# Expert products in native float32 on four column tiles of TensorE, with eight neighbouring weight rows on each partition

## The chip, the cores and the metric

One core of a Trainium2 chip runs the whole layer in one launch. The metric is the device time of one execution in microseconds (us). A core has a matrix engine (TensorE, PE in the rows; its weight loads are PEld), a vector engine (VectorE, DVE), a scalar engine (ScalarE, ACT), a general engine (GpSimd, POOL), and SyncE (SP), which here only issues DMAs. The engines meet at semaphores: an instruction adds to one when it is done, another waits until it has a value.

## The reference, cut to what matters

The layer normalises its input, runs attention and a state-space mixer side by side, projects, normalises, and then sends the tokens through an expert-choice mixture of experts. There are two sequences (256 and 512 tokens), width 1024, 16 experts of inner width 1024. Each expert picks 2 x 256/16 = 32 tokens of the first sequence and 64 of the second, 96 in all.

```python
def _expert_choice(h, w_router, w_gate, w_up, w_down):
    n_tok, d = h.shape
    cap = CAPACITY_FACTOR * n_tok // N_EXPERTS
    aff = jax.nn.softmax((h @ w_router).astype(jnp.float32), axis=-1)
    gate, idx = lax.top_k(aff.T, cap)
    xe = h[idx]
    hid = jax.nn.silu(jnp.einsum("ecd,edf->ecf", xe, w_gate)) * jnp.einsum("ecd,edf->ecf", xe, w_up)
    ye = jnp.einsum("ecf,efd->ecd", hid, w_down) * gate[..., None].astype(h.dtype)
    return jnp.zeros_like(h).at[idx.reshape(-1)].add(ye.reshape(-1, d))
```

All is float32. The weights of the experts are 16 x 3 x 4 MB = 201 MB, nearly all that the kernel reads. After the experts a per-layer embedding term and a last layer norm follow.

## The kernel before

Each engine has its own program. Up to some 620 us the layer runs up to the router, the choice of tokens and the per-layer embedding units (`ple_unit`, 12 of them, L1777); then comes the expert stage, and from 1190 us the last norm.

In the expert stage the 96 chosen rows of an expert are gathered from DRAM by GpSimd (`gather`, L635) to `xe`, turned by eight transposes on TensorE (`rows_turn`, L1865), and copied out as the stationary operand `xeT`. The weights stream past it: for each of 8 row blocks of 128 and each half of 512 columns a product of 128 x 96 by 128 x 512 is added into PSUM (`chunk`, L1873).

The products run on operands in parts. A weight piece lands in `raw` (1 MB: two row blocks, 128 x 2048); ScalarE copies it to `high` in the shorter format float32r (`split`, called through `copy`, L698), and VectorE subtracts to get `low` (`split`, L1327). The same is done to `xeT` and `hidT`. A product is then high x high, high x low and low x high: three float32r matmuls (L1880 to L1882) instead of one float32 matmul. An expert's weights are 12 pieces (4 of gate, 4 of up, 4 of down), and `raw`, `high` and `low` are rings of 6. SP loads the next piece when the split of the piece six before is done (`s_low`, L519); ScalarE splits when TensorE has used the ring's slot (`s_used`).

The order on TensorE for expert e: `gate(e)`, `hid_turn(e-1)` (eight transposes of the hidden rows), `up(e)`, `rows_turn(e+1)`, `down(e-1)`. ScalarE applies silu, VectorE multiplies gate and up (`hidden`, L1358) and scales the output by the gate value (`ye_out`, L1364, operation on L1368). GpSimd adds the 96 rows of 4 KB to DRAM (`scatter`, L656), and after the last one SP reads all back for the norm (L525 to L527).

Row `k*128 + p` of a weight matrix goes to partition p (`"e (k p) f -> e p k f"`, L496), so that a piece takes two single rows of 4 KB for each partition, 512 KB apart in DRAM.

Other products are native float32 matmuls: the per-layer units (L1792), the output projection (L1760), and the router (L1832: eight row blocks into 16 output columns, 512 and 256 moving columns).

Of the kernel before, what the change touches and what calls it, by code (L numbers as in the profile page):

```python
# [20 lines left out]
ALU = mybir.AluOpType  # L21
# [7 lines left out]
P = 128  # L29
# [17 lines left out]
NB = 6  # L47
# [18 lines left out]
def hymba_layer(nc, A, consts, out_prompt, out_sample):  # L66
# [7 lines left out]
    CAP = CAPP + CAPS  # L74
    PADW = TP * P + TS * P + 6
# [6 lines left out]
    with ctx:  # L82
# [43 lines left out]
        gateT = sb("gateT", [CAP, NE])  # L126
        idxT = sb("idxT", [CAP, NE], I32)
        idx_now = sb("idx_now", [CAP, 2], I32)
# [55 lines left out]
        xaf = xa[:, :, :].rearrange("p t c -> p (t c)")  # L184
# [16 lines left out]
        xeT = [over(f"xeT{i}", "xa", i * KD * CAP, [P, KD, CAP]) for i in range(2)]  # L201
        hidT = [over(f"hidT{i}", "xa", (2 + i) * KD * CAP, [P, KD, CAP]) for i in range(2)]
        hid = xaf[0:CAP, 4 * KD * CAP:4 * KD * CAP + D]
        ye = xaf[0:CAP, 4 * KD * CAP + D:4 * KD * CAP + 2 * D]

        CH = 2 * D
        raw = [late[:, j * CH:(j + 1) * CH] for j in range(NB)]
        where = [("ring", 4), ("ring", 8), ("xT", 0), ("xT", 4), ("ring", 0), ("mix", 0)]
        high = [over(f"high{j}", b, o * D, [P, CH]) for j, (b, o) in enumerate(where)]
        where[3] = ("gb_in", -2)  # L210
        low = [over(f"low{j}", b, (o + 2) * D, [P, CH]) for j, (b, o) in enumerate(where)]
# [97 lines left out]
        s_raw = [sem(f"s_raw{j}") for j in range(NB)]  # L309
        s_high = sem("s_high")  # L310
        s_low = sem("s_low")
        s_used = sem("s_used")
        s_xeT_h = sem("s_xeT_h")
# [3 lines left out]
        s_hT_h = sem("s_hT_h")  # L317
# [55 lines left out]
        QC = D // (2 * P)  # L373
        FIRST, PER = 2 * QC, 3 * QC

        def buf(i):
            return i % NB

        def buf0(n):
            return (n + NB - FIRST % NB) % NB  # L380

        def seq(e, i):
            return PER * e + (FIRST - PER + i)

        def landed(e, i):
            before = [buf0(n) for n in range(FIRST)].count(buf(i))
            return 16 * (PER // NB) * (e - 1) + 16 * (before + 1 + i // NB)

# [34 lines left out]
        def _(sp):  # L423
# [72 lines left out]
            wg = A["w_e_gate"][0].rearrange("e (k p) f -> e p k f", p=P)  # L496
# [3 lines left out]
            def load(j, w, e, q):  # L500
                sp.dma_start(raw[j].rearrange("p (k c) -> p k c", k=2),
                             w[e, :, 2 * q:2 * q + 2, :]).then_inc(s_raw[j], 16)
# [1463 lines left out]
```

## Time and profile before

| | |
|---|---|
| median of 3 runs | 1227.28 us (1225.72 to 1228.53) |
| span of the profiled execution | 1227.0 us |
| TensorE busy in it | 1125.2 us, 92% |
| VectorE, ScalarE, GpSimd busy | 850.3, 602.9, 364.2 us |
| moved by DMA | 253.86 MB, 207 GB/s over the span |
| mean granted clock of TensorE | 0.965 of full |

The profile follows one execution. The span goes from the first to the last instruction of it. Busy shares are means over stages that differ much, so the expert stage is read by itself below. In a timeline row the first number is the start, the second the time from the start of the group's first instruction to the end of its last, and `x8` the number of instructions in it. The end of a matmul is modelled, so its pace is read from starts.

### The profile page before, as it was taken

The numbers are of one execution on the slowest core, as the hardware profiler recorded it, in microseconds if no ns is written. First come the engines' busy times: TensorE is split into PE (matmuls) and PEld (weight loads), VectorE is DVE, ScalarE is ACT, GpSimd is POOL, SyncE is SP. The second block draws the span as 40 slices with busy tenths as digits, with TensorE's granted clock in tenths as the row PEclk, the third lists the DMA queues.
The fourth block names the chain that finished last, engine by engine and source line by source line (L and its number), as shares of the span: only waits on it lengthen the run. The fifth ranks groups of instructions, "written<-read, shape, count | busy, mean of one in ns | idle before, by whom it ended". The sixth has DMA issues, their size and how long they took to land.

```text
span 1227.0 us, 13573 instructions
## 1 busy us (share of the span) xinstructions
PE 1125.2 (92%) x4706; PEld 736.3 (60%) x4706; DVE 850.3 (69%) x1026; ACT 602.9 (49%) x741; POOL 364.2 (30%) x275
## 2 busy tenths in 40 slices
PE   5999869789998999999999999999999999999950
PEld 3568758565665454344466777777777777777630
DVE  5436783557778154273358888988888889988738
ACT  1143244456575110110256676687666776787522
POOL 0007992244544000000100333322333333322313
PEclk9999889979999999999999999999999999999985
DMA  9010100300000930200559999999999999999815
GB/s 331 6 69 4 66 1 1 103 1 1 1 1 2 317 136 35 94 26 26 175 214 332 384 382 389 390 379 390 384 395 381 385 389 395 382 386 380 311 29 202
DMA packets 74886, 253.86 MB, mean 207 GB/s; under 512 B 7384, under 2 KB 9304, under 8 KB 74848
## 3 DMA queue, kind: packets, MB, share of 16 engines
q1 hardware_dynamic: 69440, 234.49, 50.1%
q0 software_dynamic: 5408, 18.88, 5.7%
q8 instruction: 22, 0.36, 0.1%
q14 instruction: 16, 0.13, 0.0%
HBM read 237.62 MB, written 15.73 MB: 206 GB/s over the span
## 4 chain that ended last, share of the span: by engine, by line
PE 80%; DVE 9%; POOL 5%; issue 2%; ACT 2%; DMA 1%; SPq 0%; ACTq 0%; DVEq 0%; POOLq 0%
PE ps L1880 15%; PE ps L1882 14%; PE ps L1881 14%; PE ps L1792 7%; PE ps L1760 7%; PE ps L1558 4%; PE ps L1664 2%; PE ps L1679 2%; PE ps L1552 2%; PE ps L1861 2%; PE ps L1797 2%; DVE xT L1451 1%; DVE ring L1206 1%; PE ps L1790 1%; PE ps L1655 1%
## 5 line engine op out<-in xcount | busy, mean ns | idle before, releaser
L1327 DVE TENSOR_TENSOR low<-late,high 128x2048 fp32r<-128x2048 f32 x192 | 427.1, 2283 | 31.5 <-ACT high L698 31.5
L698 ACT ACTIVATE high<-late 128x2048 fp32r<-128x2048 f32 x192 | 354.9, 1914 | 24.0 <-DMA late<-in_w_e_up 23.7
L661 POOL COPY idx_now<-idxT 96x1 int32 (+1 forms) x30 | 132.7, 4423 | 375.3 <-DVE xa L1368 203.2
L1880 PE MATMUL ps<-high,xeT 128*96 128x512 f32 x528 | 210.8, 399 | 6.8 <-issue 4.8
L1882 PE MATMUL ps<-high,xeT 128*96 128x512 f32 x528 | 208.9, 396 | 0.0
L1881 PE MATMUL ps<-low,xeT 128*96 128x512 f32 x528 | 208.4, 395 | 0.0
L1880 PEld LDWEIGHTS ps<-high,xeT 128*96 128x96 f32 x528 | 86.0, 163 | 43.3 <-issue 6.1
L1882 PEld LDWEIGHTS ps<-high,xeT 128*96 128x96 f32 x528 | 85.9, 163 | 37.7 <-issue 0.5
L1881 PEld LDWEIGHTS ps<-low,xeT 128*96 128x96 f32 x528 | 86.0, 163 | 36.3 <-issue 0.3
L1880 PE MATMUL ps<-high,hidT 128*96 128x512 f32 x240 | 95.5, 398 | 2.3 <-DVE low L1327 2.3
L1882 PE MATMUL ps<-high,hidT 128*96 128x512 f32 x240 | 94.2, 393 | 0.0
L1881 PE MATMUL ps<-low,hidT 128*96 128x512 f32 x240 | 94.0, 392 | 0.0
L1792 PE MATMUL ps<-ring,xT 128*128 128x512 f32 x192 | 85.6, 599 | 0.0
L1792 PEld LDWEIGHTS ps<-ring,xT 128*128 128x128 f32 x192 | 35.5, 190 | 49.3 <-issue 49.3
L698 ACT ACTIVATE xT<-ps 128x512 f32<-128x512 f32 (+1 forms) x48 | 22.3, 512 | 70.2 <-PE ps L1773 43.2
L1285 DVE TENSOR_TENSOR mix<-mix,ps 128x512 f32<-128x512 f32 x12 | 8.2, 687 | 67.7 <-ACT mix L892 67.6
L698 ACT ACTIVATE hidT<-ps 128x384 fp32r<-128x384 f32 x30 | 13.1, 489 | 84.1 <-PE ps L1861 84.1
L822 ACT ACTIVATE ring<-ps,att 128x512 f32<-128x512 f32 (+1 forms) x48 | 29.4, 612 | 48.9 <-DVE att L1175 48.8
L892 ACT ACTIVATE mix<-ps 128x512 f32<-128x512 f32 x12 | 7.2, 597 | 93.2 <-PE ps L1797 93.2
L1880 PEld LDWEIGHTS ps<-high,hidT 128*96 128x96 f32 x240 | 38.7, 161 | 18.2 <-DVE low L1327 2.8
L1882 PEld LDWEIGHTS ps<-high,hidT 128*96 128x96 f32 x240 | 38.7, 161 | 16.9
L1881 PEld LDWEIGHTS ps<-low,hidT 128*96 128x96 f32 x240 | 38.8, 162 | 15.5
(255 smaller groups left out, 1858.1 us busy)
## 6 DMA issues: line engine op xcount, KB each, us to landing
late<-in_w_e_gate SPq DMA_DIRECT2D x64, 1024.0 KB, 6.9
late<-in_w_e_up SPq DMA_DIRECT2D x64, 1024.0 KB, 8.0
late<-in_w_e_down SPq DMA_DIRECT2D x64, 1024.0 KB, 8.1
ring<-in_w_in SPq DMA_DIRECT2D x3, 2048.0 KB, 9.1
ring<-in_w_ple_gate SPq DMA_DIRECT2D x2, 2048.0 KB, 11.5
ring<-in_w_in SPq DMA_DIRECT2D x3, 1024.0 KB, 13.0
x_rows<-xa POOLq DMA_DIRECT2D x6, 512.0 KB, 2.9
acc_rows<-mix POOLq DMA_DIRECT2D x12, 256.0 KB, 2.3
```

Of the source, the lines that this page charges most:

```text
L661: return nc.gpsimd.tensor_copy(idx_now[:, col:col + 1], idxT[:, bass.ds(e, 1)])
L698: return nc.scalar.activation(o, i, ACT.Copy)
L822: nc.scalar.activation(prob[:, u % 4, 0:L], ps[:, u % 3, 0:L], ACT.Exp, bias=att[:, 0, u:u + 1], scale=HD ** -0.5, accum_out=att[:, 1, u:u ...
L1327: nc.vector.tensor_tensor(low[j], raw[j], high[j], ALU.subtract).then_inc(s_low, 1)
L1552: last = nc.tensor.matmul(bank[:, 0:272], lhs[k], wkv[:, k, :], start=(k == 0), stop=(k == KD - 1))
L1558: last = nc.tensor.matmul(bank, lhs[k], slotk[0][:, k, :], start=(k == 0), stop=(k == KD - 1))
L1664: last = nc.tensor.matmul(ps[:, 4, :], kvd[:, a + b, P:2 * P], probT[G % 2][:, b, :], start=(b == 0), stop=(b == n - 1))
L1760: last = nc.tensor.matmul(ps[:, 4 + 2 * (t % 2) + h, :], lhs, w[:, k, :], start=(k == 0), stop=(k == KD - 1))
L1792: nc.tensor.matmul(ps[:, b, :], xT[:, k, t * P:(t + 1) * P], w[:, k, :], start=False, stop=(k == KD - 1))
L1880: nc.tensor.matmul(o, lhs[0][:, k, :], high[j][:, c], start=(k == 0), stop=False)
L1881: nc.tensor.matmul(o, lhs[0][:, k, :], low[j][:, c], start=False, stop=False)
L1882: last = nc.tensor.matmul(o, lhs[1][:, k, :], high[j][:, c], start=False, stop=(k == KD - 1))
```

## The change

The three parts, both splits and the rings go. Gate, up and down are native float32 products. The 96 tokens are three groups of 32. A product takes 32 tokens as the stationary operand and writes 32 PSUM partitions, `32*j` to `32*j+31`; j = 0..3 stands for the quarter of the inner width (or of the output width) that it computes, so that four products of a group write four column tiles of the array. Gate and up of a quarter are one product of 2 x 256 = 512 moving columns; down has 256.

The hidden rows so lie as 128 partitions (quarter, token) x 3 groups x 256, and six full transposes turn them. The output lies the same way, hence 3 scatters of 128 rows of 1 KB for each expert (`acc_quarters`), with indices `4*token + quarter` made for it (`idx4`, `jcol`) by 24 small products with the identity, beside the one transpose for the gather's indices.

Gate and up weights go to the partitions by eight neighbouring rows (row `8*p + k`), and `rows_turn` takes every eighth column of the gathered rows to match. Weights land in six slots of 2 MB: four hold a quarter of the row blocks of gate and up, two hold a half of down. SP loads into a slot when the products that used it are done (`s_ug`, `s_ud`).

Before the stage, the last per-layer unit writes its second product to bank 1 and waits for one more sum. ScalarE and VectorE keep silu, the copies out of PSUM, the product and the scaling.

```diff
-        CH = 2 * D
-        raw = [late[:, j * CH:(j + 1) * CH] for j in range(NB)]
-        high = [over(f"high{j}", b, o * D, [P, CH]) for j, (b, o) in enumerate(where)]
-        low = [over(f"low{j}", b, (o + 2) * D, [P, CH]) for j, (b, o) in enumerate(where)]
+        acc_quarters = acc_rows.rearrange("t (j c) -> (t j) c", j=CT)
+        gu_w = [slot[j].rearrange("p (w k c) -> p w k c", w=2, k=2) for j in (3, 4, 5, 0)]
+        dn_w = [slot[j].rearrange("p (k c) -> p k c", k=4) for j in (1, 2)]
...
-            wg = A["w_e_gate"][0].rearrange("e (k p) f -> e p k f", p=P)
-            wu = A["w_e_up"][0].rearrange("e (k p) f -> e p k f", p=P)
+            wg = A["w_e_gate"][0].rearrange("e (p k) f -> e p k f", p=P)
+            wu = A["w_e_up"][0].rearrange("e (p k) f -> e p k f", p=P)
             wd = A["w_e_down"][0].rearrange("e (k p) f -> e p k f", p=P)
+            def load_gu(e, q):
+                for i, w in enumerate((wg, wu)):
+                    sp.dma_start(gu_w[q][:, i], w[e, :, 2 * q:2 * q + 2, :]).then_inc(s_guw[q], 16)
+            def load_dn(e, d):
+                sp.dma_start(dn_w[d], wd[e, :, 4 * d:4 * d + 4, :]).then_inc(s_dnw[d], 16)
             sp.wait_ge(s_gs, NG)
-            for n in range(NB):
-                load(buf0(n), (wg, wu)[n // QC], 0, n % QC)
+            for q in range(3):
+                load_gu(0, q)
             sp.wait_ge(s_o, NT)
             sp.dma_start(slotk[2], wpg[:, :, 512:D]).then_inc(s_slot[2], 16)
+            load_gu(0, 3)
+            sp.wait_ge(s_pg, NT)
+            load_dn(0, 0)
...
+            sp.wait_ge(s_pg, 2 * NT)
+            load_dn(0, 1)
             for q in range(QC):
-                sp.wait_ge(s_low, seq(NE, q) - NB + 1)
-                load(buf(q), wd, NE - 1, q)
+                sp.wait_ge(s_ug, q + 1)
+                load_gu(1, q)
+            with sp.Fori(2, NE) as e:
+                for q in range(QC):
+                    sp.wait_ge(s_ug, 4 * (e - 1) + q + 1)
+                    load_gu(e, q)
+                for d in range(2):
+                    sp.wait_ge(s_ud, 2 * (e - 2) + d + 1)
+                    load_dn(e - 1, d)
...
             def scatter():
-                pool.indirect_dma_start(acc_rows, bass.IndirectOffsetOnAxis(ap=idx_now[:, 1:2], axis=0),
-                                        ye, None, compute_op=ALU.add).then_inc(s_scat, 16)
+                for i in range(NG3):
+                    pool.indirect_dma_start(acc_quarters,
+                                            bass.IndirectOffsetOnAxis(ap=idx_now[:, 1 + i:2 + i], axis=0),
+                                            ye[:, i, :], None, compute_op=ALU.add).then_inc(s_scat, 16)
...
             def ye_out(e, at_e, first=False):
+                dve.wait_ge(s_ud, 2 * (e + 1))
                 if not first:
-                    dve.wait_ge(s_scat, 16 * e)
+                    dve.wait_ge(s_scat, 16 * NG3 * e)
+                for i in range(NG3):
+                    last = nc.vector.tensor_scalar(ye[:, i, :], ps[:, DN + i, 0:256], gate4[:, i, at_e], None,
+                                                   ALU.mult)
...
+                if u == 2 * NT - 1:
+                    pe.wait_ge(s_base, u)
...
+            for v, src in enumerate((topf, topv)):
+                for i in range(NG3):
+                    c = (1 + v * NG3 + i) * NE
+                    for j in range(CT):
+                        last = nc.tensor.matmul(ps[32 * j:32 * (j + 1), 5, c:c + NE], src[:, i * 32:(i + 1) * 32],
+                                                ident[0:NE, 0:NE], start=True, stop=True)
...
-                        nc.tensor.matmul(o, lhs[0][:, k, :], high[j][:, c], start=(k == 0), stop=False)
-                        nc.tensor.matmul(o, lhs[0][:, k, :], low[j][:, c], start=False, stop=False)
-                        last = nc.tensor.matmul(o, lhs[1][:, k, :], high[j][:, c], start=False,
-                                                stop=(k == KD - 1))
+            def gate_up(e):
+                pe.wait_ge(s_xeT, e + 1)
+                if not isinstance(e, int) or e:
+                    pe.wait_ge(s_hid, e)
                 for q in range(QC):
+                    pe.wait_ge(s_guw[q], 32 * (e + 1))
+                    for i in range(2):
+                        k = 2 * q + i
+                        for g in range(NG3):
+                            for j in range(CT):
+                                last = nc.tensor.matmul(
+                                    ps[32 * j:32 * (j + 1), GU + g, :].rearrange("p (w c) -> p w c", w=2),
+                                    xeT[:, k, 32 * g:32 * (g + 1)],
+                                    gu_w[q][:, :, i, 256 * j:256 * (j + 1)], start=(k == 0), stop=(k == KD - 1))
+                    last.then_inc(s_ug, 1)
+
+            def down_half(e, d, src):
+                pe.wait_ge(s_dnw[d], 16 * (e + 1))
+                for i in range(4):
+                    k = 4 * d + i
+                    for g in range(NG3):
+                        for j in range(CT):
+                            last = nc.tensor.matmul(ps[32 * j:32 * (j + 1), DN + g, 0:256],
+                                                    src[:, k, 32 * g:32 * (g + 1)],
+                                                    dn_w[d][:, i, 256 * j:256 * (j + 1)],
+                                                    start=(k == 0), stop=(k == KD - 1))
+                last.then_inc(s_ud, 1)
...
             with pe.Fori(2, NE - 1) as e:
-                gate(e)
+                pe.wait_ge(s_xeT, e + 1)
                 hid_turn(e - 1)
-                up(e)
+                gate_up(e)
                 pe.wait_ge(s_hT, e)
                 rows_turn(e + 1)
-                down(e - 1)
+                down(e - 1, hidT)
```

The order for expert e is now `hid_turn(e-1)`, `gate_up(e)`, `rows_turn(e+1)`, `down(e-1)`.

## Rows read from the trace of the kernel before

**Rows 1.** The page: the chain that ended last, by engine and by line.
```profile
PE 80%; DVE 9%; POOL 5%; issue 2%; ACT 2%; DMA 1%; SPq 0%; ACTq 0%; DVEq 0%; POOLq 0%
PE ps L1880 15%; PE ps L1882 14%; PE ps L1881 14%; PE ps L1792 7%; PE ps L1760 7%; PE ps L1558 4%; PE ps L1664 2%; PE ps L1679 2%; PE ps L1552 2%; PE ps L1861 2%; PE ps L1797 2%; DVE xT L1451 1%; DVE ring L1206 1%; PE ps L1790 1%; PE ps L1655 1%
```
**Rows 2.** Window: length; busy PE, PEld, DVE, ACT, POOL; clock, DMA, GB/s.
```profile
760.00:770.00 10.00, 10.00 (x50) 7.19 (x49) 6.45 (x6) 6.42 (x6) 4.12 (x2) 1.00 1.03 384
```
**Rows 3.** The page's groups: the two splits of the weights.
```profile
L1327 DVE TENSOR_TENSOR low<-late,high 128x2048 fp32r<-128x2048 f32 x192 | 427.1, 2283 | 31.5 <-ACT high L698 31.5
L698 ACT ACTIVATE high<-late 128x2048 fp32r<-128x2048 f32 x192 | 354.9, 1914 | 24.0 <-DMA late<-in_w_e_up 23.7
```
**Rows 4.** Timeline of TensorE, steady part: products, then eight transposes.
```profile
1142.57 0.39 PE L1881 MATMUL ps<-low,xeT 128*96 128x512 f32 x1
1142.80 0.39 PE L1882 MATMUL ps<-high,xeT 128*96 128x512 f32 x1
1143.03 0.82 PE L1861 MATMUL ps<-cst,xa 96*128 96x96 f32 x8
1143.63 0.46 PE L1880 MATMUL ps<-high,xeT 128*96 128x512 f32 x1
```
**Rows 5.** Timeline of SP: the gate loads of two experts, one after the other.
```profile
762.79 11.63 SPq L501 DMA_DIRECT2D late<-in_w_e_gate  x4
...
797.36 11.63 SPq L501 DMA_DIRECT2D late<-in_w_e_gate  x4
```
**Rows 6.** The router's float32 products: their piece of the chain, then weight loads (timeline).
```profile
501.07 10.42 PE ps L1832 x32
...
501.44 0.10 PEld L1832 LDWEIGHTS ps<-xT,wr 128*16 128x16 f32 x1 [0.33 <-issue]
501.87 0.10 PEld L1832 LDWEIGHTS ps<-xT,wr 128*16 128x16 f32 x1 [0.33 <-issue]
```
**Rows 7.** Timeline of weight loads: eight of 6-column transposes, and the next.
```profile
86.52 0.57 PEld L1500 LDWEIGHTS ps<-cst,late 6*128 6x128 f32 x8 [0.36 <-issue]
87.10 0.19 PEld L1531 LDWEIGHTS ps<-xh_a,wh 128*128 128x128 f32 x1
```
**Rows 8.** Waits of the SP queue: line, who, us in total, times, longest.
```profile
SPq L501 <- DVE low L1327: 549.2, 186, 95.5
```
**Rows 9.** Windows, columns as above: 2 KB rows, 4 KB rows, scatter, gather.
```profile
412.00:414.00 2.00, 2.00 (x6) 0.91 (x5) 0.00 (x0) 0.00 (x0) 0.00 (x0) 1.00 1.08 373
...
930.00:932.00 2.00, 2.00 (x10) 1.39 (x9) 2.00 (x2) 0.62 (x1) 2.00 (x1) 1.00 1.03 412
...
942.00:944.00 2.00, 2.00 (x10) 1.42 (x9) 2.00 (x2) 2.00 (x2) 0.00 (x0) 1.00 1.04 281
...
956.00:958.00 2.00, 2.00 (x11) 1.37 (x10) 2.00 (x2) 2.00 (x2) 0.00 (x0) 1.00 1.03 315
```
**Rows 10.** Timeline of GpSimd: issue of a scatter.
```profile
936.33 1.46 POOL L657 DMA_INDIRECT acc_rows<-xa,idx_now  x1 [0.80 <-POOL idx_now L661]
```
**Rows 11.** The stage's start in the timeline; then the chain's last scaling.
```profile
612.33 0.69 DVE L1286 SCALAR_TENSOR_TENSOR mix<-xa,mix 128x512 f32<-128x512 f32 x1
...
619.55 1.88 PE L1797 MATMUL ps<-gb_in,kvd 128*128 128x512 f32 x4
...
620.87 0.80 PE L1880 MATMUL ps<-high,xeT 128*96 128x512 f32 x1
...
1187.75 1.29 DVE xa L1368
```
**Rows 12.** Timeline of TensorE after a wait, and the window around it.
```profile
646.28 0.55 PE L1880 MATMUL ps<-high,xeT 128*96 128x512 f32 x1 [2.02 <-DVE xeT L1347]
646.62 0.63 PE L1881 MATMUL ps<-low,xeT 128*96 128x512 f32 x1
647.05 0.63 PE L1882 MATMUL ps<-high,xeT 128*96 128x512 f32 x1
...
645.00:650.00 5.00, 3.72 (x10) 2.47 (x10) 4.80 (x5) 5.00 (x4) 0.97 (x1) 0.66 0.97 350
```

More of the change, by code:

```diff
@@ L308, in hymba_layer @@
         s_xeT = sem("s_xeT")
[L309 to L313, printed above, removed]
+        s_guw = [sem(f"s_guw{q}") for q in range(4)]
+        s_dnw = [sem(f"s_dnw{d}") for d in range(2)]
+        s_ug = sem("s_ug")
+        s_ud = sem("s_ud")
         s_hs = sem("s_hs")
@@ L368, in hymba_layer, with gate_bank, p_bank @@
             n0 += n - 1
[L373 to L387, printed above, removed]
+        def gate_bank(u):
+            return 2 * (u % 2)
+        def p_bank(u):
+            return 1 if u == 2 * NT - 1 else 2 * (u % 2) + 1
+        GU, DN, TURN = 3, 0, 6
         DT, ANEG, ACUM, EA, WDEC, CD, W1, W2 = range(8)
@@ L939, in silu, with rows_out @@
-            def silu(e, first=False):
-                act.wait_ge(s_used, (QC if first else seq(e, QC)))
-                nc.scalar.activation(hid, ps[0:CAP, 0:2, :].rearrange("p b c -> p (b c)"),
-                                     ACT.Silu).then_inc(s_hs, 1)
+            def rows_out(e):
+                act.wait_ge(s_xeT_p, e + 1)
+                for half in range(2):
+                    last = copy(xeT[:, 4 * half:4 * half + 4, :],
+                                ps[:, TURN + half, 0:4 * CAP].rearrange("p (k c) -> p k c", k=4))
+                last.then_inc(s_xeT, 1)
@@ L956, in _ @@
[L956 to L970 removed]
+            rows_out(0)
+            sigmoid(2 * NT - 1)
@@ L971, in _ @@
+            silu(0)
+            rows_out(1)
             with act.Fori(1, NE - 1) as e:
[L972 to L974 removed]
                 silu(e)
[L976 to L983 removed]
@@ L1425, in stats_half @@
+            ye_out(0, slice(0, 1), first=True)
+            with dve.Fori(2, NE) as e:
+                hid_out(e - 1, hidT)
+                hidden(e)
+                ye_out(e - 1, bass.ds(e - 1, 1))
+            hid_out(NE - 1, xeT)
+            ye_out(NE - 1, slice(NE - 1, NE))
             def stats_half(t, half):
@@ L1886, in gate @@
-            def gate(e):
+                for i in range(NG3):
+                    for b in range(2):
+                        last = nc.tensor.transpose(ps[:, TURN + b, i * P:(i + 1) * P],
+                                                   hid[:, i, b * P:(b + 1) * P], ident)
+                last.then_inc(s_hT_p, 1)
+            def gate_up(e):
                 pe.wait_ge(s_xeT, e + 1)
-                pe.wait_ge(s_hs, e)
+                if not isinstance(e, int) or e:
+                    pe.wait_ge(s_hid, e)
@@ L1898, in down @@
+            def down(e, src, mid=None):
                 pe.wait_ge(s_hT, e + 1)
-                if not first:
+                if not isinstance(e, int) or e:
                     pe.wait_ge(s_ye, e)
-                for q in range(QC):
-                    if q == QC // 2 and mid:
-                        mid()
-                    chunk(hidT, 4, q, buf(2 * QC + q), seq(e + 1, 2 * QC + q))
-            pe.wait_ge(s_idx, 2)
+                down_half(e, 0, src)
+                if mid:
+                    mid()
+                down_half(e, 1, src)
```

287 lines of the change are left out of this document (71 added, 216 removed).

## The prediction

> **What bounds the kernel now.** The chain of waits on the page comes first: 80% of it is TensorE, and the three product lines of the experts (L1880 to L1882) hold 43% of the span, some 528 us [rows 1]. Read next what the expert stage looks like in ten-microsecond stretches: TensorE is busy for all 10 us at full clock, and the DMA engines are at a share of 1.03 as well [rows 2]. So two resources are full at once, and whichever stays full after the change decides. VectorE and ScalarE are busy, but not full, and the page's groups say with what: 192 splits of 2.28 us and 192 copies of 1.91 us [rows 3]. They end no wait of TensorE in the steady part. The timeline of TensorE gives the price of a product: 0.23 us from one to the next, and eight transposes in 0.60 us [rows 4]. The loads of one expert follow those of the expert before by 34.57 us [rows 5]. An expert has 8 row blocks x 2 halves x 3 weights x 3 parts = 144 products: 144 x 0.2295 = 33.05 us, two sets of transposes 1.20, together 34.25; 0.32 us is left over. TensorE's own work sets the period, with the DMA queue close behind.
>
> **Products of the change.** For gate and up an expert gets 8 x 3 x 4 = 96 products of 512 columns, for down 96 of 256. They are native float32. What such a product costs is seen at the router: its 16 products are 32 records in 10.42 us; the loads of the 512-column ones stand 0.43 us apart [rows 6]. So one product is two records, one after the other: 2 x 0.43 = 0.86 us at 512 columns, and (10.42 - 16 x 0.43)/16 = 0.22 us a record, 0.43 us a product, at 256. Served one at a time, an expert would be 96 x 0.86 + 96 x 0.43 = 123.8 us. No row shows products of different column tiles next to each other: the router's 16 output columns all lie in one tile, and its records don't overlap. So the cost is bounded by 123.8 us (nothing overlaps) and 123.8/4 = 31.0 us (four tiles always run together). I take 31.0: the four products of a group write four different quarters of the output and share no weights in the array, and adjacent records on this engine already run back to back without a gap [rows 4, 6]. This is the choice on which all else hangs; the rivals hold the other ends.
>
> A second floor is the spacing of small pairs of load and product: eight transposes of 6 columns take 0.58 us until the next load, 0.072 us a pair [rows 7], with 128-column loads where the change loads 32. Four tiles together ask for a pair each 0.43/4 = 0.107 us (gate and up) and 0.054 us (down). By that floor the 192 down pairs cost up to 13.8 instead of 10.3 us, so 0 to 3.5 us per expert; I take 0.5, since the load of 16 columns is 0.10 us against 0.19 of 128 [rows 6, 7].
>
> Transposes: eight stay (0.60), the other eight become six (0.45). Kept change-overs 0.32. Period of TensorE: 31.0 + 0.5 + 1.05 + 0.32 = 32.9 us against 34.57.
>
> **What leaves the other engines.** The 384 splits and copies go, with all the ring's waits on L1327. They are worth nothing by themselves, as TensorE did not wait for them in steady state. The wait of SP moves from the split to the consuming products (s_ug, s_ud): now 549 us of SP's waiting ends with a split [rows 8]. The new buffers hold six pieces of 2 MB, a whole expert, instead of six of 1 MB, so a load is issued as much as one expert ahead. Queued behind each of SP's new waits are the later loads only; the order of loads is that of use.
>
> **DMA.** An undisturbed stretch moves 412 GB/s in rows of 4 KB; 2 KB rows moved 373; the stretches with the scatter and the gather fall to 281 and 315 [rows 9]. With 16 engines a 4 KB row costs 159 ns and a 2 KB row 88, so 71 ns per 2 KB and 17 ns fixed; by the same line an 8 KB row would cost 302 ns, 434 GB/s (an estimate; no row is that long). Gate and up are 8.39 MB an expert: 20.4 us now, 19.3 by that line, so 0 to 1.1 us saved; I take 0.5. If the 8 KB are still moved as two rows, nothing is saved. The scatter goes from 96 rows of 4 KB to 384 of 1 KB: 288 more pieces on 16 engines at 17 ns are 0.3 us; if its slow stretch of some 3 us goes by pieces, it is 4 x 3 = 12 us, 9 more. I take 0.3, the price of short rows seen elsewhere. The DMA need is at most 34.57 us now (share near 1), 34.4 after. TensorE at 32.9 would outrun it, but starts with expert 0 and half of its down weights already in place: from 621 us on 190.8 MB remain, 15.2 experts' worth, 15.2 x 34.4 = 523 us, to about 1149 with 5 us of gaps at the start. POOL issues three scatters of 1.46 us [rows 10] instead of one, 2.9 us more in a period where it idles.
>
> [...]
>
> **The sum**, against the profiled execution's span, 1227.0 us (the median of the runs is 1227.28, so no correction). The products of the experts start at 620.8 us [rows 11]. 24 small products for the indices and gates by quarter, two records each: 48 x 0.072 = 3.5 us, to 624.3. The last per-layer unit now waits for one more sum of VectorE before its second product; that sum ends at 613.0 and the product starts at 619.55 [rows 11], so 6 us cover it. 16 x 32.9 = 526.4, to 1150.7. Gaps: after expert 0 TensorE waits for the copy of the next rows (table load, silu and copy, some 3 us), which nothing covers now that gate and up are one stretch; a 2 us wait brought the granted clock to the 1.2 GHz level and products to 0.43 us for over 3 us [rows 12], so 5 us in all; before the last expert's down the scaled output must leave the banks, 2 us: 1157.7. DMA (1149 and the last half's products, 5 us) ends at 1154, just under it. The tail from the last scaling at 1187.75 to the end is 39.3 us [rows 11]; two more scatters add 2.9. 1157.7 + 39.3 + 2.9 = 1200 us. Ends of this case: without the small-pair floor (16 x 0.5 = 8) and without the gaps and index products (7 + 3.5) some 1180; with the floor in full (16 x 3.0 = 48 more), 1248.
>
> **Rivals.** *Two at a time (slower).* The two records of a float32 product use the same column tile and stand next to each other. If records start in program order, the second waits for the first and holds back the next tile; only the second of one product and the first of the next overlap. Then a product costs one record's time: 96 x 0.43 + 96 x 0.215 = 61.9 us, period 63.3, 16 x 63.3 = 1013 instead of 526: 1200 + 487 = 1687 us. For it: every pair of records in the trace starts in order and 0.43 us apart [rows 6]. Against it: those use one tile, so the trace can't tell. It decides as soon as fewer than 123.8/(34.57 - 1.4), i.e. 3.7 of four tiles, run together. The Trainium skill, "TensorE: Matmul & The Clock Gate", section "Part 3: Packing small matmuls — row/col tiling", says that matmuls keep program order in start and end, which is this rival's rule, and that tiles in different columns overlap. By its measured 3.07 for four tiles the sum would be near 1335 us.
>
> *Three of four together.* Loads or drains at the changes between tiled products and transposes keep a quarter of the array empty: 123.8/3 = 41.3, period 42.7, 1200 + 16 x 9.8 = 1357 us.
>
> *DMA gets slower.* The scatter by pieces (9 us more), period 43.4: 15.2 x 43.4 = 660, 1333 us; from 2.5 us more per expert on (15.2 x 2.5 = 38) the gain is gone. Half of that price gives about 1265.
>
> *Nothing overlaps*: 125.2 us a period, 16 x 92.3 more: 2677 us.
>
> **How the numbers follow.** Four together 0.60 (0.56 of it below 1224.8, 0.04 within 0.2%, which is about what a measurement of this kernel can tell from no change); two at a time 0.22; three of four 0.11; slower DMA 0.05; no overlap 0.02. Faster 0.56, same 0.04, slower 0.40. The likeliest case's own range is 1180 to 1248; with three of four and slower DMA it reaches 1357 but leaves out 0.24, so the range takes in two at a time: 1180 to 1690. What it leaves out is no overlap, and less than 1180.
>
> **What would show it.** The records of neighbouring tiles: four starts within a few tens of ns of each other, then a step of 0.43 us, means four together; starts 0.2 us apart or a step of 0.43 us per product means two. The period between the loads of two experts: 33 to 35 us is my case, 43 is three of four or a slow scatter (told apart by TensorE's idle time waiting for loads), 63 two at a time. VectorE and ScalarE must fall by 427 and 355 us. GB/s in undisturbed stretches: 412 means that long rows change nothing, 430 that they help, and less that the new row order hurts. TensorE's granted clock must stay at the 2.4 GHz level in the steady part. I am wrong if TensorE waits for loads in most of the experts or if its products are less dense than 0.107 us each.

## The result and the profile after

The changed kernel takes 1200.11 us (median of four runs, 1199.09 to 1200.78) against 1227.01 us of the kernel before in the same comparison: a ratio of 0.9779, 95% interval 0.9765 to 0.9793. The profiled execution has a span of 1198.8 us. Forecast were 1200 us.

The page of the kernel after first: busy times, packets, the chain that ended last (by engine, by line) and the groups of the expert products.

```profile
PE 1096.5 (91%) x8561; PEld 562.2 (47%) x8561; DVE 406.8 (34%) x835; ACT 236.3 (20%) x517; POOL 287.5 (24%) x311
...
DMA packets 63117, 253.98 MB, mean 212 GB/s; under 512 B 7384, under 2 KB 15448, under 8 KB 46688
...
PE 80%; DVE 9%; POOL 6%; issue 2%; ACT 2%; DMA 1%; SPq 0%; DVEq 0%; POOLq 0%; ACTq 0%
PE ps L1775 28%; PE ps L1787 14%; PE ps L1675 7%; PE ps L1643 7%; PE ps L1441 4%; PE ps L1547 2%; PE ps L1562 2%; PE ps L1435 2%; PE ps L1682 2%; PE ps L1753 1%; DVE xT L1334 1%; DVE ring L1151 1%; PE ps L1761 1%; PE ps L1673 1%; PE ps L1538 1%
...
L1775 PE MATMUL ps<-late,mix 128*32 128x512 f32 x2304 | 250.5, 593 | 0.0
L1787 PE MATMUL ps<-ring,mix 128*32 128x256 f32 x3072 | 171.1, 382 | 2.6 <-DVE mix L1280 2.6
L1775 PE MATMUL ps<-ring,mix 128*32 128x512 f32 x768 | 85.3, 592 | 0.0
```

The chain reads as before [rows 1]: 80% TensorE, and two lines where there were three: 42% of the span where it was 43%. The two groups of splits [rows 3] have no counterpart any more. VectorE's busy time fell by 443.5 us and ScalarE's by 366.6. The three product groups wait 2.6 us in all, once, at the end of the stage. A record is one entry that the trace has for TensorE, and a float32 product is two records: 96 x 2 x 16 = 3072 at each size (2304 + 768 at 512 columns). The packets of 8 KB or more are 63117 - 46688 = 16429: the 16384 long rows of gate and up do go as one packet each.

Next the timeline of TensorE for one steady expert (start, length, line, operation, tiles, count), where [rows 4] stood.

```profile
897.67 1.13 PE L1753 MATMUL ps<-cst,mix 96*128 96x96 f32 x8
898.73 10.57 PE L1787 MATMUL ps<-ring,mix 128*32 128x256 f32 x192
909.23 0.87 PE L1761 MATMUL ps<-cst,mix 128*128 128x128 f32 x6
910.03 15.66 PE L1775 MATMUL ps<-late,mix 128*32 128x512 f32 x144
925.51 5.33 PE L1775 MATMUL ps<-ring,mix 128*32 128x512 f32 x48
930.77 1.13 PE L1753 MATMUL ps<-cst,mix 96*128 96x96 f32 x8
```

And the timeline of the weight loads in its gate and up products, to be laid beside those of the router [rows 6]; a count of 4 is four loads close together.

```profile
917.36 0.13 PEld L1775 LDWEIGHTS ps<-late,mix 128*32 128x32 f32 x4 [0.30 <-issue]
917.78 0.13 PEld L1775 LDWEIGHTS ps<-late,mix 128*32 128x32 f32 x4 [0.30 <-issue]
918.21 0.13 PEld L1775 LDWEIGHTS ps<-late,mix 128*32 128x32 f32 x4 [0.30 <-issue]
```

Four loads at once, then a step of 0.43 us: four tiles run together, as long as the products last. From start to start the expert is 1.06 us of transposes, 10.50 of down products, 0.80 of transposes and 20.74 of gate and up, together 33.10 us.

Last the windows of the stage (length; busy PE, PEld, DVE, ACT, POOL; clock, DMA share, GB/s), to be laid beside [rows 2].

```profile
720.00:820.00 100.00, 100.00 (x1206) 41.89 (x1202) 9.45 (x18) 5.05 (x9) 18.04 (x18) 1.00 1.03 390
...
1020.00:1120.00 100.00, 100.00 (x1206) 41.89 (x1202) 9.45 (x18) 5.05 (x9) 16.88 (x16) 1.00 1.03 395
```

TensorE is still busy for the whole of each window at full clock, and the DMA engines are still full. VectorE and ScalarE are busy for a tenth of it or less, where it was two thirds.

### The profile page after: what moved, and what is told of

It is laid out like the page before. It is cut to its first block, busy times and chain, and to the rows that moved or that the text cites. A ratio compares the mean times of both kernels' runs of the same rounds, so it can differ in the third digit from the quotient of the medians.

```text
span 1198.8 us, 20163 instructions
## 1 busy us (share of the span) xinstructions
PE 1096.5 (91%) x8561; PEld 562.2 (47%) x8561; DVE 406.8 (34%) x835; ACT 236.3 (20%) x517; POOL 287.5 (24%) x311
## 2 busy tenths in 40 slices
DMA packets 63117, 253.98 MB, mean 212 GB/s; under 512 B 7384, under 2 KB 15448, under 8 KB 46688
## 4 chain that ended last, share of the span: by engine, by line
PE 80%; DVE 9%; POOL 6%; issue 2%; ACT 2%; DMA 1%; SPq 0%; DVEq 0%; POOLq 0%; ACTq 0%
PE ps L1775 28%; PE ps L1787 14%; PE ps L1675 7%; PE ps L1643 7%; PE ps L1441 4%; PE ps L1547 2%; PE ps L1562 2%; PE ps L1435 2%; PE ps L1682 2%; PE ps L1753 1%; DVE xT L1334 1%; DVE ring L1151 1%; PE ps L1761 1%; PE ps L1673 1%; PE ps L1538 1%
## 5 line engine op out<-in xcount | busy, mean ns | idle before, releaser
L1775 PE MATMUL ps<-late,mix 128*32 128x512 f32 x2304 | 250.5, 593 | 0.0
L1787 PE MATMUL ps<-ring,mix 128*32 128x256 f32 x3072 | 171.1, 382 | 2.6 <-DVE mix L1280 2.6
L1775 PEld LDWEIGHTS ps<-late,mix 128*32 128x32 f32 x2304 | 73.2, 110 | 166.0 <-issue 166.0
L1787 PEld LDWEIGHTS ps<-ring,mix 128*32 128x32 f32 x3072 | 98.8, 111 | 69.4 <-DVE mix L1280 3.1
L1286 DVE TENSOR_TENSOR mix<-mix,ps 128x768 f32<-128x768 f32 x16 | 15.3, 955 | 318.6 <-ACT mix L926 318.6
L1675 PE MATMUL ps<-ring,xT 128*128 128x512 f32 x192 | 85.6, 599 | 0.0
L1775 PE MATMUL ps<-ring,mix 128*32 128x512 f32 x768 | 85.3, 592 | 0.0
L658 POOL DMA_INDIRECT acc_rows<-mix,idx_now x48 | 74.9, 1561 | 20.5 <-POOL idx_now L666 10.7
L663 POOL COPY idx_now<-idxT 96x1 int32 (+1 forms) x14 | 2.5, 180 | 217.7 <-PE ps L1753 217.7
L1775 PEld LDWEIGHTS ps<-ring,mix 128*32 128x32 f32 x768 | 25.0, 110 | 57.4 <-issue 57.4
L1524 PE MATMUL ps<-xT 128*128 128x512 f32 (+1 forms) x96 | 45.0, 555 | 1.3 <-issue 1.3
L1441 PE MATMUL ps<-ring,xT 128*128 128x512 f32 x96 | 45.2, 626 | 1.2 <-ACT xT L703 1.2
L1415 PE MATMUL ps<-xl,wh 128*128 128x512 f32 (+1 forms) x128 | 44.0, 344 | 0.0
L1643 PE MATMUL ps<-ring,xT 128*128 128x512 f32 x96 | 43.2, 592 | 0.0
```

The costliest lines, as they stand in the source:

```text
L658: pool.indirect_dma_start(acc_quarters, bass.IndirectOffsetOnAxis(ap=idx_now[:, 1 + i:2 + i], axis=0), ye[:, i, :], None, compute_op=ALU.a ...
L1415: nc.tensor.matmul(o, w_h, xl[:, k, a * P:(a + w) * P], start=False, stop=False)
L1441: last = nc.tensor.matmul(bank, lhs[k], slotk[0][:, k, :], start=(k == 0), stop=(k == KD - 1))
L1524: nc.tensor.matmul(ps[:, u % 3, 0:n * P], qT[:, h % 4, t * P:(t + 1) * P], kz[:, h // 4, a * P:(a + n) * P], start=True, stop=True).then_i ...
L1643: last = nc.tensor.matmul(ps[:, 4 + 2 * (t % 2) + h, :], lhs, w[:, k, :], start=(k == 0), stop=(k == KD - 1))
L1675: nc.tensor.matmul(ps[:, b, :], xT[:, k, t * P:(t + 1) * P], w[:, k, :], start=False, stop=(k == KD - 1))
```

## The experiments

### What runs together: two tiles, one tile, no tiles

The four products of a group are put into two column tiles, or into one; all else stays. (First and last product of a tile set `start` and `stop`.)

```diff
-  ps[32 * j:32 * (j + 1), GU + g, :]
+  ps[32 * (j % 2):32 * (j % 2) + 32, GU + g, :]      # one tile: ps[0:32, GU + g, :]
```

> The four products of a group are put into two column tiles (0, 1, 0, 1) instead of four, with the same sizes, loads and order; the output of two weight quarters is summed in one place, so the expert layer's result is not the reference's. Theory A (what runs together is what lies in different column tiles, and each tile takes its records one after the other): 123.8 / 2 = 61.9 us of products, period 64, 1200 + 16 x 30.9 = about 1695 us. Theory B (the gain comes from the narrow weight load or from back-to-back native products, whatever tile they lie in): it stays near 1200 us.

> All products of the experts are put into column tile 0, with the same sizes, loads and order; the four weight quarters are summed in one place, so the expert layer's result is not the reference's. Theory A: nothing overlaps, a product is 2 x 0.43 us at 512 columns and 2 x 0.215 at 256, 123.8 us of products an expert, period 126, 1200 + 16 x 92.8 = about 2685 us; this would also confirm the price of a product read from the router. Theory B as in the kernel with two tiles: near 1200 us.

And the products in native float32 without tiles, 96 tokens in each:

```diff
-  for g in range(NG3):
-      for j in range(CT):
-          matmul(ps[32 * j:32 * (j + 1), GU + g, :], xeT[:, k, 32 * g:32 * (g + 1)], gu_w[q][:, :, i, 256 * j:256 * (j + 1)])
+  for w in range(2):
+      for h in range(2):
+          matmul(ps[0:CAP, 2 * w + h, :], xeT[:, k, :], gu_w[q][:, w, i, 512 * h:512 * (h + 1)])
```

> One part alone: native float32 without parts and splits, with the new weight rows and loads, but no column tiles: all 96 tokens in one product, 32 products of 512 columns for gate and up and 16 for down, scatter of whole rows, no index products. Theory A (a native product costs two records of 0.43 us whatever the number of its output rows; the tiles are what makes it pay): 48 x 0.86 = 41.3 us, two sets of transposes 1.2, change-overs 0.3, period 42.8, about 1200 + 16 x 9.7 = 1350 us, slower than the kernel before. Theory B (leaving out the splits and their waits is itself the gain): 1200 to 1227 us.

Measured, one run of each: two tiles 1695.7 us, one tile 2685.9, no tiles 1353.9 (the kernel before beside them: 1228.95). All three came out within 4 us of theory A. The timeline of weight loads shows why. With two tiles:

```profile
865.15 0.12 PEld L1775 LDWEIGHTS ps<-late,mix 128*32 128x32 f32 x2 [0.31 <-issue]
865.58 0.12 PEld L1775 LDWEIGHTS ps<-late,mix 128*32 128x32 f32 x2 [0.31 <-issue]
```

With one tile:

```profile
865.22 0.11 PEld L1775 LDWEIGHTS ps<-late,mix 128*32 128x32 f32 x1 [0.32 <-issue]
865.65 0.11 PEld L1775 LDWEIGHTS ps<-late,mix 128*32 128x32 f32 x1 [0.32 <-issue]
```

Without tiles:

```profile
905.04 0.16 PEld L1767 LDWEIGHTS ps<-ring,mix 128*96 128x96 f32 x1 [0.27 <-issue]
905.47 0.16 PEld L1767 LDWEIGHTS ps<-ring,mix 128*96 128x96 f32 x1 [0.27 <-issue]
```

The step is 0.43 us in every kernel; what changes is how many records share it: four, two, one. An expert's period is 33.10, 64.03 and 125.94 us with four, two and one tiles. Less the 1.86 us of transposes that is 31.24, 62.17 and 124.08: the overlap of four tiles is 3.97, of two 2.00. Without tiles a record of 96 output rows costs the same 0.43 us as one of 32, the period is 42.7 us, and the kernel is 10% slower than before. So native float32 alone loses; the four tiles win.

### Does the order of the tiles matter?

Three products of one tile in a row (all token groups of a weight quarter), then six (both row blocks of a piece as well):

```diff
-  for g in range(NG3):
-      for j in range(CT):
+  for j in range(CT):
+      for g in range(NG3):
```

> The products of one column tile come three in a row (tile 0 for tokens 0-31, 32-63, 64-95, then tile 1, ...) instead of one after the other over the four tiles. Theory A (each column tile works through its own products and the engine hands out instructions ahead of those that still run): the same four tiles run together, period 33 us, about 1200 us. Theory B (instructions start strictly in program order, and the changed kernel is fast only because its neighbours lie in different tiles): the six records of a tile start 0.43 us apart and only the last overlaps the first of the next tile, so 12 products take 20 x 0.43 = 8.6 us instead of 2.6; an expert takes 103 us of products, period 105, 1200 + 16 x 72 = about 2350 us. A time in between means that the engine looks ahead by a few instructions only.

> Six products (12 records) of one column tile in a row. Three in a row gave 2.9 records at a time in place of four. Theory A (the engine works ahead within a window of 10 to 12 records, whatever their tiles): 2.0 records at a time, 123.8 / 2 + 2 = 64 us a period, about 1695 us. Theory B (each tile takes four records ahead, one running and three behind it, and a fifth stops the engine): with three in a row that gives 3.0 as well, but now 12 records cost 9 - 1 = 8 steps a tile, 1.5 at a time, 82.5 + 2 us a period, about 2020 us.

Measured, one run of each: 1432.0 and 2080.6 us. The first lies between its two theories. Its weight loads on the timeline:

```profile
905.39 0.17 PEld L1775 LDWEIGHTS ps<-late,mix 128*32 128x32 f32 x4 [0.29 <-issue]
905.85 0.14 PEld L1775 LDWEIGHTS ps<-late,mix 128*32 128x32 f32 x2 [0.29 <-issue]
906.28 0.17 PEld L1775 LDWEIGHTS ps<-late,mix 128*32 128x32 f32 x4 [0.29 <-issue]
906.74 0.14 PEld L1775 LDWEIGHTS ps<-late,mix 128*32 128x32 f32 x2 [0.29 <-issue]
```

Those of the kernel with six in a row:

```profile
903.60 0.14 PEld L1775 LDWEIGHTS ps<-ring,mix 128*32 128x32 f32 x3 [0.32 <-issue]
904.03 0.14 PEld L1775 LDWEIGHTS ps<-ring,mix 128*32 128x32 f32 x2 [0.29 <-issue]
904.46 0.14 PEld L1775 LDWEIGHTS ps<-ring,mix 128*32 128x32 f32 x2 [0.29 <-issue]
904.91 0.11 PEld L1775 LDWEIGHTS ps<-ring,mix 128*32 128x32 f32 x1 [0.32 <-issue]
...
907.06 0.14 PEld L1775 LDWEIGHTS ps<-ring,mix 128*32 128x32 f32 x3 [0.32 <-issue]
```

Three products in a row are six records: six loads in two steps (0.89 us), three records at a time. Six in a row: 12 loads in 3.46 us or eight steps, 1.5 at a time. One rule accounts for both: a tile has one record running and up to three waiting, and the next record for a full tile stops the engine for all tiles. It is inferred from these counts; no row shows a queue. A run of six then holds the engine for 6 - 4 = 2 steps, a run of twelve for 8. A window of 10 to 12 records over all tiles would have given the second kernel a period of 64 us; it has 88.1. (Theory B's 84.5 left out that by this rule the last tile of each stretch runs its last four steps alone: 4 x 0.43 + 4 x 0.215 = 2.6 us more. With that and the 1.86 us of transposes the rule gives 45.8 and 87.0 us for the two periods, where 47.8 and 88.1 were measured: 2 and 1 us stay open.) Strict program order, theory B of the first kernel, would have given that kernel 105 us. In the changed kernel the tiles alternate after two records, which this depth covers.

### The weight rows alone

```diff
-  wg = A["w_e_gate"][0].rearrange("e (p k) f -> e p k f", p=P)
+  wg = A["w_e_gate"][0].rearrange("e (k p) f -> e p k f", p=P)
...
-  xe[:, j:D:KD]
+  xe[:, j * P:(j + 1) * P]
```

(and `wu` likewise.) The yardstick beside it was the changed kernel without an edit:

> The changed kernel once more, without an edit, as the yardstick of the three others on the same chip: 1200 us, within 1 us.

> Undoes one part: each partition gets the gate and up weights of rows 128 apart again (4 KB pieces instead of 8 KB, 32 KiB pitch gone), everything else as in the changed kernel. Theory A (TensorE sets the period at 33.1 us; long rows save DMA at most 1.1 us an expert, and the loads run close behind): 1200 to 1208 us, and the latter only if DMA's need without the saving passes 33.1 us, which the issues of the loads would show by coming later from expert to expert. Theory B (the rows carry the gain): 16 x 1.1 = 18 us or more, 1218. Theory C (neighbouring rows hurt because of their pitch): it becomes faster, below 1199.

Measured: 1199.03 us for the yardstick (1198.59 to 1201.83), 1201.39 with the old rows (1200.85 to 1203.51); against the kernel before 0.9776 (0.9763 to 0.9789) and 0.9795 (0.9782 to 0.9809). The 2.4 us are at the edge of what these runs can tell. Theory A holds, and the trace shows two opposite effects inside it. Timeline of TensorE with the old rows, three places:

```profile
959.53 0.88 PE L1753 MATMUL ps<-cst,mix 96*128 96x96 f32 x8
960.34 10.57 PE L1787 MATMUL ps<-ring,mix 128*32 128x256 f32 x192
...
988.23 5.36 PE L1775 MATMUL ps<-ring,mix 128*32 128x512 f32 x48 [0.81 <-DMA ring<-in_w_e_up]
...
1143.77 5.39 PE L1787 MATMUL ps<-ring,mix 128*32 128x256 f32 x96 [2.62 <-DVE mix L1280]
1151.06 5.39 PE L1787 MATMUL ps<-ring,mix 128*32 128x256 f32 x96 [1.90 <-DMA ring<-in_w_e_down]
```

The eight transposes take 0.81 us to the next product instead of 1.06, because they read neighbouring columns and not every eighth one. The new row order costs TensorE 0.25 us an expert, and with the old one the period is 32.85 us as long as TensorE sets it. But from 988 us on its products wait for loads, seven times for up to 0.8 us, 4.4 in all, and once for 1.9 at the end: DMA has become the later one, and this takes back what the shorter transposes gain, with some 2 us on top.

### What the DMA queue alone would allow

One product in two is left out, so that TensorE comes early and only the loads are late.

```diff
-  for i in range(2):          # gate and up, row blocks of a piece
+  for i in range(1):
...
-  for i in range(4):          # down
+  for i in range(2):
```

> Half of the expert products are left out (one row block of two in gate and up, two of four in down), all loads, gathers and scatters stay: TensorE then needs some 17.6 us an expert, and what is left of the period is what the DMA queue needs. My estimate of that need was 34.4 us; the changed kernel ran at a period of 33.1 with its loads close behind, so theory A: 33.0 to 33.6 us between the loads of two experts (TensorE and DMA nearly level). Theory B: clearly less, 32 us or below, then DMA was a bystander and its late loads at the end have another cause.

> As the kernel with half of the products, but with 4 KB pieces for the gate and up weights: the difference of the two periods is what the 8 KB pieces are worth to DMA. My bounds were 0 to 1.1 us an expert and I took 0.5; undisturbed stretches of 434 against 412 GB/s speak for 1.0 (theory A), a mere 2.4 us of the whole kernel's time between the two row orders could also be 0.2 us an expert (theory B).

> As the kernel with half of the products and 8 KB pieces, but with one of the three scatters of an expert left out of three kept: one scatter of 128 pieces instead of three. The period's fall against it is the DMA price of 256 pieces of 1 KB. Theory A (17 ns a piece on 16 engines and their bytes, 256 x 64 ns / 16): about 1 us less. Theory B (the scatter's slow stretch goes by pieces; 8 us at some 345 instead of 430 GB/s, two thirds of it): 1.1 us less, hardly to be told from A. Theory C (each piece costs far more, up to the 9 us of the rival): 3 us or more.

In the last one two of the three scatters of an expert are left out, so two token groups in three don't get its output. Measured, one run of each: 1194.55, 1195.83 and 1168.68 us. The period is read from the issue of the down loads on SP's timeline; the first and the last of 13 stand here, with 8 KB pieces and three scatters:

```profile
686.80 11.15 SPq L494 DMA_DIRECT2D ring<-in_w_e_down  x2
...
1096.42 8.91 SPq L494 DMA_DIRECT2D ring<-in_w_e_down  x2
```

and with one scatter:

```profile
685.07 10.61 SPq L494 DMA_DIRECT2D ring<-in_w_e_down  x2
...
1078.60 36.19 SPq L494 DMA_DIRECT2D ring<-in_w_e_down  x4
```

(1096.42 - 686.80)/12 = 34.14 us; with 4 KB pieces by the same two rows (693.97 and 1105.62) 34.30; with one scatter 32.79. So neither theory for the first kernel is right as it stood: DMA needs 1.0 us an expert *more* than TensorE. The changed kernel runs at 33.10 us all the same, because its loads start an expert ahead and lose a microsecond of the lead with each expert. Its own trace shows that. The first down loads of experts 1 and 13 are issued at 672.62 and 1069.82 us, 33.10 us an expert; the times from issue to landing are:

```profile
DMA to landing us min/median/max: 9.3/9.3/9.3
...
DMA to landing us min/median/max: 24.6/24.6/24.6
```

They land 34.37 us an expert apart, so that 15.3 us of the lead are lost in 12 experts, and the last of them lands at 1094.4 us, 2.9 us before TensorE starts on it (1097.33). The lead lasts just to the end of the 16 experts.

The 390 GB/s of the changed kernel (window 720:820 above) are those of the queue working without a pause: the kernel with half of the products, which waits for loads everywhere, has the same in that window.

```profile
720.00:820.00 100.00, 60.35 (x583) 22.12 (x574) 9.41 (x18) 4.90 (x9) 17.07 (x17) 0.93 1.03 390
```

By the issues, eight-KB pieces are worth 0.17 us an expert; but in the kernels with half of the products an issue can itself be held up (one at 1071.8 us takes 3.6 us where 0.4 is usual), and the landings of the same loads (first half of down, experts 1 to 13) are steadier. They are 34.14 us apart with 8 KB and 34.45 with 4 KB pieces, and 34.37 and 34.60 in the changed kernel and the one with the old rows. So the pieces are worth 0.2 to 0.3 us an expert, nearer to theory B. Two scatters are worth 1.35 us by the issues and 1.31 by the landings, some 0.67 each, or 84 ns of one engine for a piece of 1 KB (0.67 x 16 / 128). Theories A and B both lie near, C is out. (Theory A's 64 ns a piece has no working: 17 ns and 71 per 2 KB give 53 ns, and 0.85 us for the two.)

At the end of this kernel TensorE's timeline reads:

```profile
1138.39 4.40 PE L1787 MATMUL ps<-ring,mix 128*32 128x256 f32 x48 [5.00 <-DMA ring<-in_w_e_down]
1145.25 4.39 PE L1787 MATMUL ps<-ring,mix 128*32 128x256 f32 x48 [2.45 <-DMA ring<-in_w_e_down]
```

The last weights are there at 1145 us. That is what the loads allow in this order of issue; halving TensorE's work brings no more than 5.6 us. (The 48 records take 4.40 us here and 2.80 elsewhere in this run: in the waits the granted clock falls, to 0.66 of full in the window 1145:1150. Some 1.6 us of the last products are due to that and not to the loads.)

### The work of the splits put back beside the path

```diff
+  for i in range(12):   # ScalarE, in each expert of the loop
+      act.wait_ge(s_dua, 12 * e + i)
+      copy(xa[:, 2:4, :], xa[:, 0:2, :]).then_inc(s_dua, 1)
...
+  for i in range(8):    # VectorE
+      dve.wait_ge(s_dud, 8 * (e - 1) + i)
+      nc.vector.tensor_tensor(xa[:, 4:6, :], xa[:, 0:2, :], xa[:, 0:2, :], ALU.subtract).then_inc(s_dud, 1)
```

> Puts work of the size of the splits back where nothing waits for it: in each expert of the loop ScalarE makes 12 copies of 2048 columns (1.9 us each, 23 us) and VectorE 8 subtractions of 2048 columns (2.3 us each, 18 us), on scratch data. Theory A (the splits were worth nothing by themselves; TensorE's own products set the period): 1200 us, within 1 us, with VectorE and ScalarE busier by some 255 and 320 us. Theory B (the busy engines slowed TensorE or the DMAs, by memory or by late copies): 1205 us or more.

Measured: 1199.17 us (1198.99 to 1200.43) against 1199.03 of the yardstick; ratio to the kernel before 0.9775 (0.9762 to 0.9788). The page's busy times of this kernel, and its group of scatter issues:

```profile
PE 1095.8 (92%) x8561; PEld 562.6 (47%) x8561; DVE 663.4 (55%) x955; ACT 558.5 (47%) x697; POOL 324.4 (27%) x311
...
L660 POOL DMA_INDIRECT acc_rows<-mix,idx_now x48 | 111.8, 2329 | 20.5 <-POOL idx_now L668 10.7 <-issue 9.8
```

257 us more on VectorE and 322 on ScalarE, of the 444 and 367 that the change took away, cost nothing. Theory A holds: taking work off these two engines was not the gain.

### The end of the stage

```diff
 # SP: the last expert's down weights go where its own first gate and up pieces lay
-  sp.wait_ge(s_ud, 2 * (NE - 2) + d + 1)
-  load_dn(NE - 1, d)
+  sp.wait_ge(s_ug, 4 * (NE - 1) + d + 1)
+  sp.dma_start(dn_last[d], wd[NE - 1, :, 4 * d:4 * d + 4, :]).then_inc(s_dnl[d], 16)
 # TensorE: its products go into the banks of gate and up, without the wait for s_ye
-  down(NE - 1, xeT)
+  pe.wait_ge(s_hT, NE)
+  pe.wait_ge(s_hid, NE)
+  for d in range(2):
+      down_half(NE - 1, d, xeT, GU, dn_last, s_dnl)
 # VectorE: the last hid_out ahead of the scaling of the expert before
+  hid_out(NE - 1, xeT)
   ye_out(NE - 2, slice(NE - 2, NE - 1))
-  hid_out(NE - 1, xeT)
```

> The end of the expert stage alone: the last expert's down weights go into the slots that its own gate and up products free, so their loads are issued some 16 us earlier, its down products go into other banks and need not wait until the output of the expert before is scaled, and its transposed values are copied out before that scaling. In the changed kernel the last expert's down products wait 2.6 us for VectorE and last 12.4 instead of 10.6 us because the second half waits for its load. Theory A (these waits are on the path): 3 to 4.5 us less, about 1196. Theory B (the DMA queue is behind by then, so that earlier issues change nothing): 1198.5 to 1200.

Measured: 1195.17 us (1193.70 to 1196.62), ratio to the kernel before 0.9738 (0.9724 to 0.9751); 3.9 us under the yardstick. TensorE's last down products in the kernel after:

```profile
1135.36 5.39 PE L1787 MATMUL ps<-ring,mix 128*32 128x256 f32 x96
1143.36 12.38 PE L1787 MATMUL ps<-ring,mix 128*32 128x256 f32 x192 [2.62 <-DVE mix L1280]
```

and in this one:

```profile
1135.53 5.39 PE L1795 MATMUL ps<-ring,mix 128*32 128x256 f32 x96
1140.73 10.54 PE L1795 MATMUL ps<-late,mix 128*32 128x256 f32 x192
```

Both waits are gone, theory A holds, and this version beats both kernels.

The 12.38 us in the kernel after are not only a wait for a load, as the expectation has it. Its window with the granted clock (the third number from the end), and the weight loads of the last half:

```profile
1145.00:1147.00 2.00, 2.00 (x24) 1.09 (x20) 0.00 (x0) 0.00 (x0) 1.70 (x2) 0.50 1.01 389
...
1150.35 4.91 PEld L1787 LDWEIGHTS ps<-ring,mix 128*32 128x32 f32 x96 [0.40 <-DMA ring<-in_w_e_down]
```

After the wait of 2.62 us the granted clock fell to its 1.2 GHz level, four records took 0.43 instead of 0.21 us, and the first half was only just done when the load of the second landed (1150.3). In the kernel with the old rows the first half took its 5.39 us after the same wait, and TensorE then waited 1.90 us for the load. So the load sets these 1.8 us, and the slow clock is hidden behind it.

The load is late because it is issued late, not because the queue is behind. Window 1130:1135 of the kernel after, then window 1140:1145 of this version:

```profile
1130.00:1135.00 5.00, 5.00 (x92) 2.96 (x85) 0.95 (x1) 1.60 (x2) 0.00 (x0) 1.00 0.08 32
...
1140.00:1145.00 5.00, 5.00 (x100) 2.99 (x93) 1.27 (x3) 0.00 (x0) 2.10 (x3) 1.00 0.23 81
```

In the first the DMA engines are all but idle, as the last two loads wait for their slots. In this version the last weights land at 1143.3 us, and TensorE runs without a pause until 1151.3: what is left here is TensorE's own work, with the loads two to three microseconds ahead of it. That the kernel with half of the products is only a microsecond faster does not speak against this, since it issues its last loads late as the kernel after does.

## Why the prediction came out

The forecast of 1200 us and the mechanism held; term by term:

- **Four tiles together, the choice on which all hung:** right. 31.24 us of products were measured, 31.0 + 0.5 predicted. Each end had its own kernel: one tile 2685.9 us (the rival that nothing overlaps: 2677), two tiles 1695.7 (two at a time: 1687). So the rivals' prices were right and their condition was wrong: a record waits for the record before it in its own tile, not for the one before it in the program. The page "TensorE: Matmul & The Clock Gate" of the Trainium skill, section "Part 3: Packing small matmuls — row/col tiling", has program order for start and end, and 3.07 for four tiles. The trace does not agree: the overlap here is 3.97, and records of other tiles do overtake, up to the depth that the kernels with three and six in a row show. That 3.07 of the Trainium skill is for row tiles, while the change uses column tiles; for these the section lists three tiles at 2.38. (With the prediction's other terms the sum by 3.07 is 1341 us, not 1335.)
- **Price of a product, 0.86 us read from the router:** right, also with 96 rows (no tiles: 1353.9 us).
- **Floor of small pairs, 0 to 3.5 us, 0.5 taken:** there is none at this size. 192 down pairs took 10.50 us, 0.055 a pair, where the transposes of 6 columns [rows 7] had shown 0.072. Why those were slower was not tried.
- **Transposes 1.05 and change-overs 0.32 us:** too small. Up to the next product they take 1.06 + 0.80 = 1.86. Six transposes of 128 rows were taken as six eighths of eight of 96, and the read of every eighth column, which the new row order forces, was costed at nothing; the experiment with the old rows puts it at 0.25 us an expert, 4 us in all. This is the step that was mis-sized most in the period: 33.10 for 32.9.
- **DMA, 34.4 us an expert, hidden by the lead:** right, measured 34.14. (Between landings it is 34.37 in the changed kernel itself.) Its parts were less good. Long rows 0.2 to 0.3 for 0.5 us. Undisturbed stretches did reach 434 GB/s (window 896:898 of the kernel after), but most of the 1.1 us that this promised did not show in the period. That the rows of the partitions now lie 32 KiB apart did no harm. The scatter's pieces cost 84 ns instead of the 53 that the line of 17 ns and 71 per 2 KB gives, or 2.0 us for three; 96 rows of 4 KB at the weights' 159 ns would be 0.95, so it is some 1.1 us more where I took 0.3 and bounded by 9. The last landing, 1149 us by the estimate, comes at 1145 in the kernel with half the products, and at 1150.3 in the changed kernel, where the last load is not issued before 1140.8.
- **Index products 3.5 us, gap after expert 0 5 us:** both too large. The expert products start at 621.60 instead of 624.3, since 48 records in small tiles took 0.6 us; the gap was 0.96 us, and the granted clock stayed at its 2.4 GHz level, so the fall that [rows 12] shows after a 2 us wait did not come here. It came after the 2.62 us wait at the end of the stage, where the sum had no term for it.
- **Before the last down 2 us, tail 42.2:** measured 2.62 and 43.0. Not foreseen were 1.8 us before the last half, which are set by its late load; the prediction had DMA end just under TensorE.
- **Span and time:** I set them equal. The profiled execution of after took 1200.75 us for its span of 1198.8, so the sum of 1200 us of span stood for some 1202 of time.

The misses are 3 us up (period, 16 x 0.2), 7 down (start and gap) and 3 up (end), and 2 more for span and time: that forecast and median agree to 0.1 us is partly their cancelling, and the period is the better witness for the working.

That the splits were worth nothing by themselves, and that the extra wait of the last per-layer unit costs nothing, both held. The gain is small because the native products in four tiles are not much cheaper than the three parts: 31.24 us an expert against 33.05, some of it lost again in longer transposes, so that the period went from 34.57 to 33.10 us. That is 23.5 of the 28.2 us between the two spans; the rest is the balance of the stage's two ends and the tail, and was not taken apart. DMA's need stands at 34.14, so that only the lead of the loads lets the shorter period be had at all.

## What to carry to other kernels

Float32 products in different column tiles ran fully in parallel here, with the program handing them out in turn; count the records per tile and divide, and do not put more than a few of one tile in a row. A product split into parts for speed is worth comparing with the native one in tiles. For 96 tokens, 128 rows and 512 columns that is 3 parts x 0.23 = 0.69 us against 3 groups of 32 x 0.86 / 4 = 0.65. With 128 tokens, four groups, the tiles would cost 0.86 and lose (an estimate from the same prices; no run has it). Where two resources are within 5% of each other, measure each alone (halve the products, leave out the scatter) before working on either.

## What the runs showed of the hardware

- The depth of the queue per column tile: one record running and three waiting, inferred from runs of 2, 6 and 12 records, with 1 to 2 us of the periods left open; other lengths of run were not tried.
- A record of float32 takes 0.43 us at 512 columns with 32 or 96 output rows alike (weight loads 0.43 us apart with one tile and without tiles).
- The read of every eighth column makes eight 96 x 96 transposes 0.25 us longer (1.06 against 0.81).
- After the same wait of 2.62 us TensorE's granted clock fell to its 1.2 GHz level in the kernel after (0.50 in the window 1145:1147), while in the kernel with the old rows the products kept their full pace (96 records in 5.39 us).
- GpSimd's issue of a scatter went from 1.56 to 2.33 us while VectorE and ScalarE were kept busy on scratch data (lines L658 and L660, 48 each); which of the two does it was not tried, and it cost no time here.
